# Moving the first conv tap, two state copies and the turned-block copies of an SSD mixer from ScalarE to VectorE

## The reference

```python
zxbcdt = u @ w_in
z = zxbcdt[..., :SSD_D_INNER]
xbc = silu(dwconv_centred(zxbcdt[..., SSD_D_INNER:SSD_D_INNER + SSD_CONV_DIM], conv_w, conv_b))
dt = softplus(dt_raw.reshape(b, l, 2, H) + dt_bias)
...
def dwconv_centred(u, w, b):      # K = 5 taps along the tokens
    out = b
    for k in range(K):
        out = out + w[k] * up[:, k:k + L]
...
# ssd_scan, forwards and backwards, over two chunks of 128 tokens
states = einsum('bcsgn,bcsge,bcsgep->bcgepn', Bc, decay_to_end, xdt)
h, _ = scan(lambda h, st, al: h * exp(al) + st, ...)
```

## Time and profile before

| | us |
|---|---|
| median of 3 runs | 3088.58 (3088.0 to 3089.89) |
| the profiled execution's own time | 3088.0 |
| its span | 3085.1 |
| SSD mixer in it, from the first context block to the last before the next feed-forward part | 435 to 843 |
| of this, context and latent projections with the states and turns | 435 to 690 |

### The profile page before, as it was taken

One profiled execution on the slowest core, in us unless ns is written; L12 is line 12 of the kernel. 1 busy time (PEld: TensorE's weight loads), 2 busy tenths in 40 slices (PEclk: granted clock), 3 DMA queues, 4 the chain that ended last, 5 costly groups with the idle time before them and its releaser, 6 DMA issues.

```text
span 3085.1 us, 37413 instructions
## 1 busy us (share of the span) xinstructions
PE 2604.5 (84%) x13854; PEld 1978.6 (64%) x13854; DVE 2183.9 (71%) x3896; ACT 1074.0 (35%) x2248; POOL 738.9 (24%) x683
## 2 busy tenths in 40 slices
PE   7999999998999999899876788767786788876656
PEld 5999998886899899899762355324553245532212
DVE  6886866649368878678228766797667966689675
ACT  4434333324243434433322333223432244332221
POOL 0000000005000000000004434344433443344553
PEclk9999999999999999999888898999899998999878
DMA  7766963330369689389449999999999999999997
GB/s 311 266 231 239 369 241 140 112 134 2 130 237 363 258 316 365 138 329 360 161 146 420 409 418 409 420 419 419 421 421 420 411 407 400 420 422 421 421 419 325
DMA packets 137015, 977.06 MB, mean 317 GB/s; under 512 B 15517, under 2 KB 15525, under 8 KB 18992
## 3 DMA queue, kind: packets, MB, share of 16 engines
q0 software_dynamic: 91088, 661.23, 52.7%
q1 hardware_dynamic: 44496, 308.06, 26.2%
q10 hardware_dynamic: 1296, 6.04, 0.5%
HBM read 974.21 MB, written 1.06 MB: 316 GB/s over the span
## 4 chain that ended last, share of the span: by engine, by line
PE 50%; DMA 24%; DVE 14%; issue 5%; ACT 5%; POOL 1%; DVEq 0%; ACTq 0%; POOLq 0%
PE psum L625 49%; DMA rows<-in_peer,eidx 23%; DVE rows L2294 3%; DVE yacc L1587 2%; DVE arena L1732 1%; PE psum L628 1%; ACT L1132 1%; DVE wlow L1584 1%; DVE arena L1584 1%; POOL rows L2427 1%; DVE rep L2083 1%; DVE arena L1590 1%; ACT u L1132 0%; ACT dots L1132 0%; DMA arena<-in_ada_t 0%
## 5 line engine op out<-in xcount | busy, mean ns | idle before, releaser
L625 PE MATMUL psum<-rows,diag 128*128 128x512 f32 x1440 | 791.3, 692 | 347.4 <-ACT diag L1132 340.9
L2294 DVE CUSTOM_DVE_ANT_0 rows<-rows,h2tok 128x1024 f32<-128x1024 f32 x512 | 626.7, 1225 | 334.1 <-DMA rows<-in_peer,eidx 326.2
L2427 POOL DMA_INDIRECT rows<-in_peer,eidx x512 | 618.2, 1207 | 959.6 <-PE psum L625 560.7
L625 PEld LDWEIGHTS psum<-rows,diag 128*128 128x128 f32 x1440 | 292.5, 216 | 777.9 <-ACT diag L1132 493.8
L625 PE MATMUL psum<-u_hi,whigh 128*128 128x256 f32 x1760 | 505.3, 287 | 20.9 <-DVE u_lo L1587 18.1
L625 PE MATMUL psum<-u_lo,whigh 128*128 128x256 f32 x1760 | 501.6, 285 | 0.0
L625 PE MATMUL psum<-u_hi,wlow 128*128 128x256 f32 x1760 | 501.3, 285 | 0.0
L1584 DVE TENSOR_TENSOR wlow<-wring,whigh 128x2048 fp32r<-128x2048 f32 x165 | 377.1, 2289 | 120.9 <-ACT whigh L1132 115.3
L1132 ACT ACTIVATE whigh<-wring 128x2048 fp32r<-128x2048 f32 x165 | 314.1, 1908 | 173.0 <-PE psum L625 132.5
L1132 ACT ACTIVATE dots<-dots 128x2 f32<-128x2 f32 x256 | 52.2, 204 | 891.7 <-DVE dots L2294 891.5
L625 PEld LDWEIGHTS psum<-u_hi,whigh 128*128 128x128 f32 x1760 | 340.8, 194 | 24.1 <-issue 19.3
(11 more groups left out here) (274 smaller groups left out, 3231.1 us busy)
## 6 DMA issues: line engine op xcount, KB each, us to landing
arena<-in_ada_t POOLq DMA_DIRECT2D x116, 1024.0 KB, 7.5
wring<-in_ffn_w_gate SPq DMA_DIRECT2D x55, 1024.0 KB, 6.3
wring<-in_ffn_w_up SPq DMA_DIRECT2D x55, 1024.0 KB, 7.1
wring<-in_ffn_w_down SPq DMA_DIRECT2D x55, 1024.0 KB, 6.5
wring<-in_w_in SPq DMA_DIRECT2D x32, 1024.0 KB
wring<-in_peer_wq SPq DMA_DIRECT2D x32, 1024.0 KB
wring<-in_ssd_w_in SPq DMA_DIRECT2D x30, 1024.0 KB, 4.8
wring<-in_w_out SPq DMA_DIRECT2D x16, 1024.0 KB
```

Of the source, the lines that this page charges most:

```text
L625: return nc.tensor.matmul(out, lhsT, rhs, start=start, stop=stop, skip_group_check=shared)
L2294: v.tensor_tensor_reduce(out=rows[:, n % SLOTS, 0:D], in0=rows[:, n % SLOTS, 0:D], in1=h2tok[:, t, :], scale=1.0, scalar=0.0, op0=ALU.mult ...
L2427: pool.indirect_dma_start(out=rows[:, n % SLOTS, :], out_offset=None, in_=A[f"peer{u // 2}"], in_offset=bass.IndirectOffsetOnAxis(ap=eidx[ ...
```

## The change

Five things move in the instruction lists; what is computed stays the same.

- Tap 0 goes from ScalarE to VectorE, as a TENSOR_SCALAR with two per-partition operands (weight and bias). VectorE now waits for `proj_evicted` in place of `tap_ready`, and does five taps of two instructions.
- The ten copies of the latents' turned blocks go from ScalarE to VectorE: turns 0 and 1 behind conv block 9 and `sums(1)`, 2 and 3 behind conv block 10, 4 and 5 behind conv block 11, 6 to 9 behind that.
- The copies of the states k = 0 and 2 into `h_first` go from ScalarE to VectorE.
- VectorE's latent list is ordered anew: `state_end(i)` and `state_begin(i + 1)` stand behind conv block i for i = 0 to 3, and `softplus` goes on behind conv block 1 in place of 4.
- Small ones: a wait for `exp_a` by name, and a semaphore of its own for the final norm's sum in place of the shared counter.

```diff
@@ -1285,19 +1276,6 @@
                 nconv = 12 if lat else 10
-                def context_state(k):
-                    act.wait_ge(state_done, k + 1)
-                    f(h_first[:, k // 2, :], psum[:, 0:4, :].rearrange("p a b -> p (a b)"), ACT.Identity).then_inc(state_added, 1)
-                def turned(first, count):
-                    if first == 0:
-                        act.wait_ge(state_done, 4)
-                    for j in range(first, first + count):
-                        g, c = j // 2, j % 2
-                        act.wait_ge(tok_done, 10 + j + 1)
-                        f(xtok[:, c, 512 * g:512 * g + 512] if g < 4 else btok[:, c, :], bank(4 + j % 2), ACT.Identity).then_inc(tok_evicted, 1)
@@ -1313,18 +1291,6 @@
                         f(dtw[:, 0, :], dtw[:, 0, :], ACT.Exp).then_inc(expabs_ready, 1)
-                    if lat and i == 0:
-                        act.wait_ge(tok_done, 10)
-                    act.wait_ge(proj_evicted, 11 * lat + 2 + i)
-                    for b in range(2):
-                        blk = 2 * i + b
-                        ins = f(xbc[:, blk, :], raw[:, t % 3, b, 0:T], ACT.Identity, scale=col("conv_w", blk), bias=col("conv_b", blk))
-                    ins.then_inc(tap_ready, 1)
-                    if lat and i in (2, 4):
-                        context_state(i - 2)
-                    if lat and i >= 8:
-                        turned(2 * i - 16, 2)
                     if i:
@@ -1821,28 +1796,37 @@
                 for i in range(12 if lat else 10):
                     t = 10 * lat + i
-                    dve.wait_ge(tap_ready, t + 1)
-                    for k in range(1, CONV_W):
+                    dve.wait_ge(proj_evicted, 11 * lat + 2 + i)
+                    if lat and i == 0:
+                        dve.wait_ge(tok_done, 10)
+                    for k in range(CONV_W):
                         for b in range(2):
                             blk = 2 * i + b
                             src = raw[:, t % 3, b, k:k + T]
-                            ins = stt(xbc[:, blk, :], src, col("conv_w", 24 * k + blk), xbc[:, blk, :], ALU.mult, ALU.add)
+                            w = col("conv_w", 24 * k + blk)
+                            if k == 0:
+                                ins = ts(xbc[:, blk, :], src, w, col("conv_b", blk), ALU.mult, ALU.add)
+                            else:
+                                ins = stt(xbc[:, blk, :], src, w, xbc[:, blk, :], ALU.mult, ALU.add)
                         if k < CONV_W - 1:
                             tick(ins)
...
                         else:
                             ins.then_inc(conv_done, 1)
-                    if i == (4 if lat else 1):
+                    if i == 1:
                         next(sp_steps)
+                    if lat and i < 4:
+                        state_end(i)
+                        if i < 3:
+                            state_begin(i + 1)
                     if lat:
-                        if i in (2, 4):
-                            state_end(i - 1)
-                        if 1 <= i < 4:
-                            state_begin(i)
                         if i == 7:
                             step_sizes(1)
                         if i == 9:
                             sums(1)
+                        if i >= 9:
+                            turned(1, 2 * i - 18, 2)
                     else:
                         if i == 2:
@@ -1896,19 +1880,20 @@
                 c = 1 - first_chunk(d) if second else first_chunk(d)
-                if 0 < k < 5:
-                    dve.wait_ge(state_done, k)
                 weigh(xw[:, 0, :], c, wdt[:, c, 32 * d:32 * d + 32]).then_inc(xw_ready, 1)
                 if second or k >= 4:
-                    dve.wait_ge(state_added, k)
                     tick(tt(heads3(h_state(d, k >= 4)), heads3(h_first[:, d, :]),
...
             def state_end(k):
-                dst = h_state(k // 2 if k < 4 else k - 4, k >= 4)
+                d, second = (k // 2, k % 2) if k < 4 else (k - 4, 1)
+                dst = h_state(d, k >= 4)
                 dve.wait_ge(state_done, k + 1)
-                tt(dst, dst, psum_state, ALU.add).then_inc(state_added, 1)
+                if not second:
+                    v.tensor_copy(dst, psum_state).then_inc(state_added, 1)
+                else:
+                    tt(dst, dst, psum_state, ALU.add).then_inc(state_added, 1)
                 dve.wait_ge(state_added, k + 1)
@@ -1916,6 +1901,7 @@
             ssd_conv(1)
+            turned(1, 6, 4)
             decay_weights(1)
```

## The result

| | before | after |
|---|---|---|
| median, 4 runs each side by side | 3088.29 us (3083.19 to 3089.89) | 3122.89 us (3117.55 to 3129.24) |
| ratio, 95% interval | | 1.0115 (1.0103 to 1.0128) |
| profiled execution, its own time | 3088.0 | 3122.5 |
| its span | 3085.1 | 3120.8 |

What follows compares the result with a forecast made beforehand. The prediction took TensorE, without slack from 435 to 690, as the bound: 25.0 us of waits plus 8.8 of slow clock make 33.8, so 3088.0 becomes 3121.8, predicted as 3122 us, range 3111 to 3128.

Steps and rivals of the forecast that it cites:

- TensorE has no slack from 435 to 690: Latent stage: the chain is all TensorE, which waits for nobody, so any wait there lengthens the run.
- The context blocks cost nothing: Ten context conv blocks, each 0.65 us longer on VectorE, fit into TensorE's 6.9 to 7.8 us per block: no cost.
- State wait 6.1: Latent states: VectorE's weighing for state 2 ends at 569.1, TensorE asked at 562.98, so it waits 6.1 us.
- Turn waits 6.7, 6.1 and 6.1: Behind latent blocks 10, 11 and 12: turns 2, 4 and 6 wait for copies standing behind conv blocks on VectorE.
- 25.0 us of waits in all at full clock: Latent stage: one state wait and three turn waits of TensorE, 6.1 + 6.7 + 6.1 + 6.1, all on the chain.
- Slow clock 8.8: Behind each of the four waits TensorE runs at 1.2 GHz for a while, losing 2.2 us each, 8.8 in all.
- Slow transposes, three times some 0.5 us on top: Turns behind waits: if transposes don't count as activity, eight run slow per turn wait, some 0.5 us extra each.
- Tap 0, 0.65 us a block: VectorE's conv blocks: two TENSOR_SCALARs with the wait for the second add 0.65 us, making a block 4.28 us.
- a clock that stays high: Rival: TensorE stays at 2.4 GHz behind its waits, only 25.0 us of waits remain, 3113 us; chance 0.12.
- a clock that stays low: Rival: TensorE's clock stays at 1.2 GHz until the next wait, 52.6 us in all, 3141 us; chance 0.05.
- only the state wait would count: Rival: turn copies come in time after all, leaving 6.1 + 2.2 us for the state, 3097 us; chance 0.04.
- VectorE's slack would cover everything: Rival: VectorE's idle time covers the added work, TensorE never waits, time stays 3088 to 3089 us; chance 0.03.

Runs made afterwards that it cites:

- experiment 1: Changed kernel with VectorE's copies of turns 0 to 5 ahead of conv blocks 9, 10 and 11 instead of behind them: 3096.61 us, ratio to before 1.0032.
- experiment 8: Kernel before with only tap 0 of all 22 conv blocks given to VectorE: 3089.41 us against 3088.77, ratio 1.0003.
- experiment 3: Changed kernel with turn copies 0 to 5 ahead of conv blocks 9 to 11 and softplus behind conv block 0: 3090.1 us against 3087.23, ratio 1.0008.
- experiment 7: Kernel before with only the latents' turn copies given to VectorE, behind conv blocks 9, 10 and 11: 3118.38 us, ratio 1.0097.
- Experiment 2: Changed kernel with the latents' softplus behind conv block 0 instead of conv block 1: 3118.02 us, ratio 1.0098.
- experiment 5: Changed kernel with 12 added 128x256 matmuls, results thrown away, ahead of each of TensorE's four waits: 3115.58 us, ratio 1.0091.
- experiment 6: Changed kernel with 6 added 128x256 matmuls, results thrown away, ahead of each of TensorE's four waits: 3122.22 us, ratio 1.0103.

## Why the prediction was right

- *TensorE has no slack from 435 to 690.* Right. The distance grew by what it waited and by its clock. The 1.6 us that the next stretch, up to the second norm sum, is shorter (196.26 against 197.88) are no slack that took the loss up: it is 196.28 and 196.27 too in experiments 1 and 8, with one wait or nearly none, and 197.87 and 197.90 in 3 and 7.
- *The context blocks cost nothing.* Right: no wait of TensorE there in the changed kernel, nor in experiment 8.
- *State wait 6.1.* The bracket is 6.02; from the end of the block at 558.47 + 6.91 to 571.56 it is 6.18. The chain's items were within 0.1 us each. Experiment 2 removes it by moving softplus alone, so softplus behind conv block 1 is its cause, though each item adds to it.
- *Turn waits 6.7, 6.1 and 6.1.* Experiment 5 shows the first undisturbed by the clock: from the block's end at 616.77 to the turn 6.50, and 1.07 from there to the next block against 0.87 before, 6.7 together; the other two are 0.5 less. Experiments 1 and 7 show the cause from both sides.
- *25.0 us of waits in all at full clock.* Measured by experiment 5: 25.6, of which 0.3 was lost ahead of `ssd_sums`, where VectorE's `step_sizes` came late; I had allowed up to 1 for it.
- *Slow clock 8.8.* Measured 7.9 by experiment 5. The 9.55 that the brackets leave of the distance are 9.0 of longer rows and 0.5 of edges. The nearness was in part luck: behind the four waits the rows are longer by 2.1, 3.0, 1.5 and 2.4 us, and only their mean, 2.26, is near the 2.2 that I took. The rows sum to 9.0 and not to 7.9, since at full clock some 1 us of waiting comes out that the slow rows cover (0.2 us ahead of each turn's second half, and the 0.3 ahead of `ssd_sums`). Nor did the rows ahead of the prediction promise a fixed price: the slow stretch of 6.4 us followed a wait of 4.2, the one of 4.5 a wait of 5.85.
- *Slow transposes, three times some 0.5 us on top, left out of the sum.* Eight transposes took 0.90 us longer in each turn. Whether the slow stretch is also no shorter for them the rows don't decide: with a turn at its head it lasted some 6, 3 and 5 us, with states some 4.
- *Tap 0, 0.65 us a block.* 0.77 with the hand-over. The row that I went by had one per-partition operand at 348 ns; with two it is 408.
- *The sum 33.8 and 3122 us.* 34.6 between the medians. The terms that were off, -0.9 for the clock and +0.6 for the waits, nearly cancel, and it helped that no other part differed by more than executions do.

Of the rivals, a clock that stays high is refuted by the granted clock of 0.50 behind each wait, and a clock that stays low by the 1.00 further on in the same blocks. That only the state wait would count is refuted by the three turn waits. That VectorE's slack would cover everything was true of the work (experiment 3) and false of the order, and it was the order that was changed with it.

Two things stay open. In experiment 6 the two longer idle times, 3.42 and 3.75 us, were followed by slow work and the two of 3.23 were not; with four places in one execution this doesn't show that length decided it. And the stretch up to the second norm sum has one of two lengths, near 196.3 or near 198 us, in kernels with and without the waits; I did not pursue why.

## What to carry to other kernels

Before giving a copy to an engine with idle time, find the instruction that waits for the copy and what stands ahead of the copy in the new list: if that needs the block that the waiting engine has just finished, the two take turns and overlap nothing, here with VectorE busy 42.03 us of the 90 from 600 to 690. Put such copies ahead of the block's own work, and long chains of small instructions where the engine already waits for something else. In this stage a wait of TensorE of about 6 us cost about 8.

## What the runs showed of the hardware

- A granted clock of 0.50 behind TensorE's waits added about a third to them: 7.9 us to 24.0. Adding 12 matmuls in each wait, whose results are thrown away, made the traced stage 7.9 us shorter. The Trainium skill, "TensorE: Matmul & The Clock Gate", section "What's actually happening", has the slow clock as the state that idleness brings; the traces agree at all four places of the changed kernel (0.50 or 0.51 right behind each wait).
- One 128x256 float32 matmul stands in the profile as two records of 0.216 us. Whoever counts rows counts halves: 25 instructions took 10.8 us.
- A VectorE tensor_scalar of 128x256 in float32 took 348 ns with one per-partition operand and one operation, 408 with two of each (one of 64x256 with one such operand and two operations, in softplus, 345), and a scalar_tensor_tensor of the same size 482.
- A copy of 128x2048 float32 from PSUM took VectorE 2292 ns and ScalarE 1878; of 128x512, 683 and 595.
